# Two-layer streaming encoder trunk: the seven block products of the FFN in another order, with their preparation moved

## What is computed

```python
def rmsnorm(x, g):
    return x * rsqrt(mean(x * x, -1) + 1e-6) * g
def swiglu(x, w_gu, w_down):             # D_FF = 2816
    g, u = split(x @ w_gu, 2, axis=-1)
    return (silu(g) * u) @ w_down
for l in range(2):
    x = x + 0.5 * swiglu(rmsnorm(x, norm_g[l, 0]), ffn_w_gu[l, 0], ffn_w_down[l, 0])
    x = x + mixer(rmsnorm(x, norm_g[l, 1]))
    x = x + 0.5 * swiglu(rmsnorm(x, norm_g[l, 2]), ffn_w_gu[l, 1], ffn_w_down[l, 1])
y = rmsnorm(x, final_norm_g)
```

## Time and profile before

| | |
|---|---|
| median of 3 runs (lowest, highest) | 2731.59 us (2727.64, 2732.09) |
| profiled execution: its own time, its span | 2732.55 us, 2730.8 us |
| busy: PE, PEld, DVE | 94%, 89%, 60% of the span |
| busy: ACT, POOL | 35%, 29% |
| mean granted TensorE clock | 0.959 |

### The profile page before, as it was taken

How to read it: one execution, slowest core, us unless ns; L and a number is a source line. 1 busy time by engine, 2 the same in 40 slices (tenths; PEclk the granted TensorE clock), 3 DMA queues, 4 the chain that set the end, 5 groups by cost and what they waited for, 6 DMA issues and landing times. The chain is left out here.

```text
span 2730.8 us, 46499 instructions
## 1 busy us (share of the span) xinstructions
PE 2563.3 (94%) x18787; PEld 2420.3 (89%) x18787; DVE 1651.9 (60%) x2986; ACT 960.4 (35%) x1640; POOL 793.4 (29%) x434
## 2 busy tenths in 40 slices
PE   4999999999789999999799999999888898999997
PEld 4999999998659999999799999999844488999997
DVE  7848579322345867758884857931133348848486
ACT  4414333220173433424441433321054544424242
POOL 1232323321152232333223232332233331232322
PEclk7999999999599999999899999999988999999998
DMA  3222222222351222222222222234599931222222
GB/s 110 70 86 78 78 93 63 79 76 84 127 224 63 77 70 89 76 92 66 74 70 85 78 78 93 65 111 127 215 360 369 368 141 49 76 93 70 85 71 77
DMA packets 66556, 304.20 MB, mean 111 GB/s; under 512 B 9361, under 2 KB 13218, under 8 KB 40242
## 3 DMA queue, kind: packets, MB, share of 16 engines
q1 hardware_dynamic: 66354, 301.38, 31.7%
HBM read 279.95 MB, written 21.41 MB: 110 GB/s over the span
## 5 line engine op out<-in xcount | busy, mean ns | idle before, releaser
L782 PE MATMUL ps<-xs_hi,wb_hi 128*128 128x320 f32 x2112 | 664.7, 315 | 62.3 <-DVE xs_lo L607 32.1
L782 PE MATMUL ps<-xs_lo,wb_hi 128*128 128x320 f32 x2112 | 659.6, 312 | 0.0
L782 PE MATMUL ps<-xs_hi,wb_lo 128*128 128x320 f32 x2112 | 659.5, 312 | 0.0
L362 POOL TENSOR_TENSOR w_lo<-w_raw,w_hi 128x1024 fp32r<-128x1024 f32 (+2 forms) x130 | 393.6, 3030 | 655.5 <-ACT w_hi L358 655.5
L665 POOL TENSOR_TENSOR wb_lo<-w_raw,wb_hi 128x512 fp32r<-128x512 f32 x176 | 281.4, 1601 | 954.8 <-DVE wb_lo L673 656.6
L782 PEld LDWEIGHTS ps<-xs_hi,wb_hi 128*128 128x128 f32 x2112 | 402.8, 191 | 71.8 <-DVE xs_lo L607 29.5
L782 PEld LDWEIGHTS ps<-xs_lo,wb_hi 128*128 128x128 f32 x2112 | 403.3, 191 | 0.0
L782 PEld LDWEIGHTS ps<-xs_hi,wb_lo 128*128 128x128 f32 x2112 | 403.0, 191 | 0.0
L358 ACT ACTIVATE w_hi<-w_raw 128x1024 fp32r<-128x1024 f32 (+2 forms) x130 | 158.2, 1217 | 585.7 <-PE ps L376 504.2
L376 PE MATMUL ps<-h_hi,w_hi 128*128 128x320 f32 x1408 | 321.3, 309 | 2.4 <-DVE h_lo L939 2.0
L376 PE MATMUL ps<-h_lo,w_hi 128*128 128x320 f32 x1408 | 320.8, 309 | 0.0
(11 more groups left out here) (241 smaller groups left out, 4365.6 us busy)
## 6 DMA issues: line engine op xcount, KB each, us to landing
w_raw<-in_w_up SPq DMA_DIRECT2D x87, 1024.0 KB, 4.8
kv_ring<-in_fox_kc SPq DMA_DIRECT2D x32, 1024.0 KB, 12.8
kv_ring<-in_fox_vc SPq DMA_DIRECT2D x32, 1024.0 KB, 12.7
w_raw<-in_w_in SPq DMA_DIRECT2D x24, 1024.0 KB, 4.8
w_raw<-in_w_down_a SPq DMA_DIRECT2D x32, 512.0 KB, 3.5
w_raw<-in_w_down_b SPq DMA_DIRECT2D x32, 384.0 KB, 3.0
fox_s_s<-s_bias_dram SPq DMA_DIRECT2D x16, 576.0 KB, 10.0
w_raw<-in_w_down_a SPq DMA_DIRECT2D x32, 256.0 KB, 2.6
```

The source lines that it names most:

```text
L362: nc.gpsimd.tensor_tensor(out=w_lo[:, slot, 0:cols], in0=w_raw[:, slot, 0:cols], in1=w_hi[:, slot, 0:cols].bitcast(F32), op=ALU.subtract). ...
L782: last = nc.tensor.matmul(ps[:, bank, 0:HALF], w_part[:, slot, cols], x_part[:, k, :], start=k == 0 and i == 0, stop=k == 3 and i == 2)
```

## The change

1. The products run in the order P1, P5, P2, P3, P6, P7, P4. All engines' orders follow it: DVE takes P2, P6, P5, P3, multiplies the gate, then takes P7 and P5 again, and P4 at the start of the next tile. The low part of A22 is made in its own tile, not in the tile ahead.
2. The sums S1, S2 and S4 of the first tile of a pass are made after units 4, 5 and 6 of the stage ahead (`first_blocks_dve`). The rest (`late_blocks_*`) is placed inside the preparation of the last unit, between its first and second part. `sum_x` gets a place of its own.
3. The passes are 6, 8 and 8 tiles.
4. The five norm diagonals and the copy to `inv_rms` move from DVE to ACT. The statistics products come after P3 (one product later than before), and P4, right behind the spread, waits for `inv_ready`.
5. In the first FFN the squares are taken between the other steps of ACT, and TensorE sums them: 40 statistics products instead of 5, after P5. DVE's eight additions go. The first two tiles of x are loaded ahead of the first weights, and the constants' masks are cast after the first pass.

```diff
-GROUPS = ((0, 8), (8, 16), (16, 22))
+GROUPS = ((0, 6), (6, 14), (14, 22))
-PRODUCTS = ("P1", "P5", "P6", "P2", "P7", "P4", "P3")
+PRODUCTS = ("P1", "P5", "P2", "P3", "P6", "P7", "P4")
...
-    def block_prep_dve(dve, ph, t):
-        sum_step(dve, ph, t, "S1")
-        sum_step(dve, ph, t, "S2")
-        sum_lo_step(dve, ph, t, "S1")
+    def first_blocks_dve(dve, ph, t, step):
+        if step == 0:
+            sum_step(dve, ph, t, "S1")
+        elif step == 1:
+            sum_step(dve, ph, t, "S2")
+        else:
+            sum_step(dve, ph, t, "S4")
+            sum_lo_step(dve, ph, t, "S1")
+            second_lo_step(dve, ph, t)
+    def late_blocks_dve(dve, ph, t):
+        sum_lo_step(dve, ph, t, "S4")
         sum_lo_step(dve, ph, t, "S2")
         sum_step(dve, ph, t, "S3")
-        sum_step(dve, ph, t, "S4")
-        second_lo_step(dve, ph, t)
         sum_lo_step(dve, ph, t, "S3")
...
     def ffn_stats(pe, ph):
...
         if r == 0:
             pe.wait_ge(consts_loaded, 16 * len(consts))
+            pe.wait_ge(sq_done, KT)
+            for tt in range(TT):
+                for m in range(KT):
+                    last = nc.tensor.matmul(ps[:, STATS_BANK, tt:tt + 1], first_squares[:, m, tt * P:(tt + 1) * P],
+                                            mean_model[:, :], start=m == 0, stop=m == KT - 1)
...
+    def ffn_norm_act(act, ph):
...
+        act.wait_ge(rs_step, RS_NORM0[r] + RS_OPS)
         for tt in range(TT):
-            nc.vector.tensor_scalar(out=gate[:, 1, tt * P:(tt + 1) * P], in0=ident[:, :],
-                                    scalar1=rs[1][:, tt:tt + 1], scalar2=None,
-                                    op0=ALU.mult).then_inc(diag_done, 1)
+            nc.scalar.activation(gate[:, 1, tt * P:(tt + 1) * P], ident[:, :], ACT.Copy,
+                                 scale=rs[1][:, tt:tt + 1]).then_inc(diag_done, 1)
...
-            if t == 0 and name == "P3":
+            if t == 0 and name == "P4":
                 pe.wait_ge(inv_ready, ph["index"] + 1)
...
-                    if t == 0 and name == "P6":
+                    if t == 0 and name == ("P3" if ph["norm"] else "P5"):
                         ffn_stats(pe, ph)
                     elif t == 0 and name == "P7":
                         ffn_spread(pe, ph)
...
     def ffn_pool(pool, ph):
...
             for t in range(lo, hi):
...
-                    plain_lo_step(pool, ph, t + 1, "A11")
...
-                    plain_lo_step(pool, ph, t + 1, "A22")
+                plain_lo_step(pool, ph, t, "A22")
+                if t + 1 < hi:
+                    plain_lo_step(pool, ph, t + 1, "A11")
...
     def _(act):
...
+        for m in range(4):
+            act.wait_ge(x_loaded[m // 2], 16)
+            xs_act(act, PLAN[0], m, m)
+            square(m)
+        sum_hi_step(act, PLAN[0], 0, "S1")
+        plain_hi_step(act, PLAN[0], 0, "A12")
+        late_blocks_act(act, PLAN[0], 0, None, 0)
+        for m in (4, 5):
+            act.wait_ge(x_loaded[2], 16)
+            xs_first(act, PLAN[0], m, two(m), 0)
+            square(m)
+        for m in range(4, KT):
+            xs_second(act, PLAN[0], m)
+            if m < KT - 2:
+                act.wait_ge(x_loaded[3], 16)
+                xs_first(act, PLAN[0], m + 2, two(m), lo_before(PLAN[0], m) + 1)
+                square(m + 2)
```

More of the change, by code:

```diff
@@ L162, in trunk_program @@
     tile_b = T * 4
-    inv_rms = place("inv_rms", [P, T], F32, at_e + 7 * tile_b)
+    at_inv = (end - tile_b) // 64 * 64
+    inv_rms = place("inv_rms", [P, T], F32, at_inv)
     xs = [[(place(f"xs_hi{e}", [P, 6, 4, HALF], F32R, at_xs[e]),
@@ L528, in raw_part @@
         return w_raw[:, n % 2, c0:c0 + BLOCK]
+    SUM_AT = {"S1": 1, "S2": 2, "S4": 3, "S3": 4}
+    SUM_LO_AT = {"S1": 1, "S4": 2, "S2": 3, "S3": 4}
+    PLAIN_AT = {"A11": 1, "A12": 2, "A22": 3}
     SUMS = {"S1": sum_x, "S2": sum_y, "S3": sum_x, "S4": sum_z}
@@ L568, in lo_before, with xs_dve @@
         return 16 * ph["index"] + 2 * pos
-    def xs_dve(dve, ph, m, pos):
+    def xs_dve(dve, ph, m, pos, between=None, scaled=None):
+        scaled = prod[:, 0, :] if scaled is None else scaled
         r = ph["norm"]
@@ L858, in ffn_act @@
             r = ph["norm"] + 1
+            follow = (nxt, 0) if last else (ph, hi)
+            blocks = not last or (nxt is not None and nxt["kind"] == "ffn")
             for d in range(KT):
@@ L917, in bank, with take @@
             return ps[:, bank_of(ph, t, name), 0:HALF]
-        def take(t, name, dst, src, of):
+        def take(t, name, step, dst, src, of):
             u = f0 + t
+            assert step == READ_AT[name] or name == "P5" and step == 3
             dve.wait_ge(product_done, 7 * u + AT_PRODUCT[name])
@@ L927, in take, with up_first @@
             nc.vector.tensor_tensor(out=dst, in0=src, in1=bank(t, name), op=ALU.add).then_inc(evicted, 1)
-        def second_half(t):
-            u = f0 + t
-            take(t, "P3", gate[:, t % 2, HALF:T], part[:, 2, :], 2)
-            dve.wait_ge(evicted, 7 * u + 7)
-            nc.vector.tensor_tensor(out=gate[:, t % 2, :], in0=gate[:, t % 2, :], in1=inv_rms[:, :],
-                                    op=ALU.mult).then_inc(gate_ready, 1)
+        def up_first(t):
+            take(t, "P4", 7, prod[:, t % 2, 0:HALF], part[:, 1, :], 5)
         def hidden_lo(t, lo):
@@ L997, in ffn_dve @@
             r = ph["norm"] + 1
+            follow = (nxt, 0) if last else (ph, hi)
+            blocks = not last or (nxt is not None and nxt["kind"] == "ffn")
             if last:
                 clear_sum(dve)
+            if ph["index"] == 0 and g_ == 0:
+                cast_masks(dve)
             for d in range(KT):
                 q = q0 + d
-                if d == KT - 1 and not last:
-                    block_prep_dve(dve, ph, hi)
-                elif d == KT - 1 and nxt is not None and nxt["kind"] == "ffn":
-                    block_prep_dve(dve, nxt, 0)
+                late = (lambda: late_blocks_dve(dve, *follow)) if d == KT - 1 and blocks else None
                 dve.wait_ge(unit_ready, q + 1)
@@ L2061, in _ @@
     def _(pool):
-        block_prep_pool(pool, PLAN[0], 0)
+        plain_lo_step(pool, PLAN[0], 0, "A11")
         for ph in PLAN:
```

339 lines of the change are left out of this document (170 added, 169 removed).

## The result

The changed kernel takes 2757.55 us (median of 4 runs, 2757.4 to 2758.8) against 2730.95 us of the kernel before in the same comparison: 1.01 times as long, 95% interval 1.0083 to 1.0118. Its profiled execution took 2757.69 us with a span of 2755.9 us, 25.1 us over the span of before. The forecast was 2709.

The account below looks back on a forecast made before the run. TensorE, busy 94% of the span, was taken as the bound, so only idle time and slow stretches could be won. Terms -7.7 - 3.5 - 4 - 7 + 0 = -22.2 from 2732.55 give 2710.3, as median 2709; range 2693 to 2725.

Parts of the forecast that it names:

- The terms of the starts: First tile of each FFN: 0 us at the first, -3.5 second, -7 third, -4 fourth.
- First FFN: Its first tile: eighth square at 31, 80 statistics passes of 0.213 us, end at 61.9 against 62.17: 0 us.
- rival (a): First FFN's statistics passes run at the full rate, taking another 8 us: 2701 us; chance 0.15.
- Second and fourth: First tile of these FFNs: earlier preparation and diagonals on ACT save 3.5 and 4 us, bounds 0 to -7 each.
- Third: First tile of the third FFN, DVE-bound: longer units and earlier preparation save 7 us, bounds -3 and -13.
- the one on the passes: Steady tiles: TensorE holds DVE twice per tile with 2.7 us slack, drift goes: -7.7 us, bounds 0 and -7.7.
- Rival (c): Steady tiles: POOL's A22 and A11 parts hold DVE, tile some 14 us; from 13.0 the gain is gone; chance 0.07.
- The signs named ahead: Right: 12.3 us gate product steps, no TensorE wait on `prod`. Wrong: tiles over 12.4, `inv_rms` waits, eighth square past 35.

Follow-up runs that it names:

- The run with the late sums: POOL placed, with the five early steps moved behind the last output tile's add after a mixer alone (second and fourth FFN): 2714.6 us, ratio 0.9945.
- POOL placed: Changed kernel with POOL's low parts of A22 and A11 waiting for DVE's low parts of the next S1 and S4: 2717.39 us, ratio 0.995.
- the run without the collision: POOL placed plus statistics passes run as each square arrives, with A22's low part moved from POOL to DVE: 2689.27 us, ratio 0.9843.

## Why the prediction was wrong

The terms of the starts held, with their sum of -14.5 against -15.0 measured:

- *First FFN*, 61.9 forecast: 61.18. The eighth square came at 31.62 (31 forecast), and 80 passes took 17.06 us (17.0 forecast, 0.213 each). By the Trainium skill's figure (TensorE: Matmul & The Clock Gate, section LDWEIGHTS) they would have taken 8.5 us, an estimate; the measurement sides with the row. That the clock stayed at its lower level for all of them was not certain: two later versions ran the first 3.2 to 3.5 us at the full one, as rival (a) had it for the whole.
- *Second and fourth*, -3.5 and -4: -3.5 and -4.0. The copy to `inv_rms` stands open for 1.0 us at each, as forecast (1.2). The way there held too: in the second FFN the preparation of the last output starts 4.24 us after the stage ahead ends (4.4 forecast), against 7.54 before. The run with the late sums shows that the early sums have next to no part in it (4.47 without them). What is left is the preparation in two halves, with the late block steps behind its first half, and the new order of the products; these two were not tried apart.
- *Third*, -7: -6.6. Of it the longer last pass gives 4.8, and the early sums take 2.4 back (measured with POOL placed). The forecast had seen DVE as the bound there, and did not draw the conclusion that sums put between its units push the units back.

**The step that failed is the one on the passes: -7.7 forecast, +47.3 measured.** (Its terms, 4 x 1.4 and 2.0, add to 7.6.) It said that DVE is held by TensorE twice per tile, that TensorE has 2.7 us of slack, and that the whole drift would go, with 0 as the other bound if POOL's two steps per tile "hold DVE as they do now". In the trace of after, DVE waits for nothing in a steady tile, and that bound was none. Before, POOL's timeline had the two steps here:

```profile
271.50 1.30 POOL L665 TENSOR_TENSOR wb_lo<-w_raw,wb_hi 128x512 fp32r<-128x512 f32 x1 [7.18 <-DVE wb_lo L673]
275.18 2.00 POOL L665 TENSOR_TENSOR wb_lo<-w_raw,wb_hi 128x512 fp32r<-128x512 f32 x1 [2.38 <-ACT wb_hi L656]
```

The first cost 0.50 us, on the gate product. The second cost nothing: DVE's product beside it (275.21) kept its 0.81 us while POOL's step took 2.00 instead of 1.30, and from 276.02 on it lay in DVE's wait for S1's copy. The step was costed at nothing because it was hidden, and the price without its cover was left out of the bound. In the new order the cover is gone twice: A22's high part is there as soon as the tile ahead has ended, A11's follows 0.8 us later, and both POOL steps run while DVE has a low part and a product to do: 1.48 us per tile. Nor did the forecast count the 0.63 us that DVE's own steps lose in the new order. By the sums above the collisions alone would have made 11.04 + 1.48 = 12.52 us, 0.2 over TensorE's tile; with the order it is 0.84.

Rival (c) named that mechanism, the engine and the decision point of 13.0 us, and it came true at 13.15. It was given 0.07 because S1's low part would wait for P5 at that place. In the trace POOL's steps fall on S3's low part and the hidden product, three and more steps ahead of that low part, and a wait there is gone too (240.64 follows 240.02 at once). Its sums were off in places: 11.5 and twice 1.6 are 14.7 us, not some 14, and a tile of 13.5 gives 4 x (19 x 1.19 - 8.1) = 58 us over the forecast's 2709 by its own formula, so 2767 and not 2745. Its price was also too low: 19 intervals x 0.84 less three times 2.7 is 7.9 us per FFN, while the run without the collision shows 370.41 - 357.44 = 13.0. The last tile of each pass is late too (22 tiles, not 19 intervals); with that, the slack comes to about (22 x 0.84 - 13.0) / 3 = 1.8 us, an estimate.

With the collision taken away the forecast of the passes comes back: 1430.6 us for the four stretches in the run with A22 on DVE, against 1492.7 - 4 x 14.07 = 1436.4 for the same work before, so -5.8 us. DVE has next to nothing to spare there, though (12.27 us against 12.31), since it does A22's step itself.

The signs named ahead decided it: tiles over 12.4 us and a wait of TensorE on `prod`.

## What to carry to other kernels

Before an order of steps is changed, write down beside each step of the slower helper engine which steps of the other engine run at that moment and which operands those have; a step that costs nothing today may do so only because the other engine waits there. Where an engine's tile without waits comes near the bound's (here 11.7, by the sum above, against 12.3 us), every collision of half a microsecond counts on every tile, and two semaphore waits that place a helper's step beside reads of PSUM gave back 40 us here. A gain from work done early is measured place by place: the same early sums gave 3 to 4.6 us at a pass end, 0.3 at most behind a mixer, and took 2.4 us where DVE was the bound.

## What the runs showed of the hardware

A POOL subtraction and a DVE step with both operands in SBUF do not go on together. Where POOL's had begun, the DVE step ended 0.68 us after it (199.66 and 200.34 in the version with POOL placed; 272.80 and 273.48 before), where alone it takes 0.82. The hold goes the other way too: before, DVE's product at 275.21 kept its 0.81 us and POOL's step took 2.00 instead of 1.30. A DVE step that reads PSUM beside a POOL step keeps its 0.47 to 0.49 us. The Trainium skill (SBUF — State Buffer, section "SBUF: two separate sides") says this of the port pair that the two engines have in common: it is locked for a whole instruction by whichever starts first, and a vector step with two SBUF inputs contends with a GpSimd step that reads SBUF. The trace agrees, and this rule was at hand for rival (c).

The granted clock by stretch can fail to show a slow TensorE. For the 80 passes the change has 0.50, the lower of the two levels (1.2 GHz), behind the wait of 10.7 us:

```profile
31.62:48.68 17.06, 17.06 (x80) 17.06 (x81) 9.94 (x12) 4.12 (x6) 3.40 (x2) 0.50 0.18 63
```

and the version with the statistics as the squares arrive, where they follow P5 directly, has 1.00 for passes just as slow:

```profile
21.29:38.36 17.07, 17.07 (x82) 17.07 (x82) 13.59 (x21) 12.06 (x17) 0.13 (x1) 1.00 0.00 1
```

The products behind it start 0.26 us apart (38.77 to 39.03), where 0.147 is the full rate. That trace has no record of the clock before 44 us, and the column reads 1.00 where there is none. The distance of the products says more there than the column.
